# A hybrid decoder step on one core: routing on the unnormalised rows, and a different split of the last additions

## What is computed

```
xp = xp + merge_branches(...)                       # x1: residual + output projection (@ w_out)
h  = rms_norm(xp, g_ffn) = xp * rsqrt(mean(xp^2) + eps) * g_ffn
logits = h @ w_router + b_router                    # 1024 -> 32 experts
top_v, top_e = top_k(logits, 4); gates = softmax(top_v)
y = sum over the 4 chosen experts of gate * (clamped SwiGLU(h @ w_gu[e] + b_gu[e]) @ w_down[e] + b_down[e])
xp = xp + y
y_out = rms_norm(xp, g_final)
```

## Time and profile before

| | |
|---|---|
| median of 3 runs (lowest to highest) | 1586.99 us (1584.3 to 1587.69) |
| the profiled execution, its own time | 1584.94 us |
| its span, first to last instruction | 1583.1 us |
| PE busy | 1541.8 us (97%) |
| DVE busy | 790.7 us (50%) |
| ACT busy / POOL busy | 277.6 us (18%) / 186.9 us (12%) |
| DMA | 509.52 MB, mean 322 GB/s |
| mean granted TensorE clock | 0.987 |

### The profile page before, as it was taken

How to read it: one execution, slowest core, us unless ns; L and a number is a source line. 1 busy time by engine, 2 the same in 40 slices (tenths; PEclk the granted TensorE clock), 3 DMA queues, 4 the chain that set the end, 5 groups by cost and what they waited for, 6 DMA issues and landing times.

```text
span 1583.1 us, 32897 instructions
## 1 busy us (share of the span) xinstructions
PE 1541.8 (97%) x13183; PEld 713.7 (45%) x13183; DVE 790.7 (50%) x2042; ACT 277.6 (18%) x554; POOL 186.9 (12%) x269
## 2 busy tenths in 40 slices
PE   9999999999999799999999999999999999999995
PEld 8677487777755433333333333333333333333332
DVE  4349738704523645444544454445444534453448
ACT  2310020005301111111111121111111111111113
POOL 3633410014200000000000000000000000000000
PEclk9999999999999799999999999999999999999998
DMA  6555755723170599999999999999999999999995
GB/s 238 163 166 171 254 183 172 249 84 127 40 304 29 194 376 416 417 420 410 417 414 416 413 416 416 417 403 416 415 413 402 414 415 417 406 416 417 416 400 201
DMA packets 72468, 509.52 MB, mean 322 GB/s; under 512 B 13338, under 2 KB 13786, under 8 KB 47186
## 3 DMA queue, kind: packets, MB, share of 16 engines
q1 hardware_dynamic: 62154, 489.15, 77.3%
q0 software_dynamic: 10256, 19.61, 3.6%
HBM read 497.50 MB, written 19.88 MB: 327 GB/s over the span
## 4 chain that ended last, share of the span: by engine, by line
PE 77%; DMA 17%; DVE 2%; issue 1%; ACT 1%; POOL 1%; SPq 0%; DVEq 0%; POOLq 0%; ACTq 0%
PE PS L1319 36%; PE PS L935 16%; DMA weight_ring<-w_gu 16%; PE PS L1325 7%; PE PS L1243 3%; PE PS L1331 3%; PE PS L986 2%; PE PS L1051 2%; PE PS L1037 1%; PE PS L1101 1%; PE PS L1000 1%; POOL weight_ring L629 1%; DVE weight_ring L1804 1%; PE PS L1276 1%; DMA y_k<-region_x,idx_y 1%
## 5 line engine op out<-in xcount | busy, mean ns | idle before, releaser
L1319 PE MATMUL PS<-weight_ring,region_experts 128*32 128x512 f32 x5376 | 596.9, 593 | 6.7 <-DMA weight_ring<-w_gu 5.8
L1319 PEld LDWEIGHTS PS<-weight_ring,region_experts 128*32 128x32 f32 x5376 | 170.0, 110 | 400.6 <-issue 365.2
L1738 DVE TENSOR_TENSOR region_experts<-PS,region_w 128x512 f32<-128x512 f32 x96 | 66.4, 692 | 459.1 <-PE PS L1319 459.1
L1325 PE MATMUL PS<-weight_ring,act_turned 128*32 128x512 f32 x2048 | 225.6, 592 | 0.0
L935 PE MATMUL PS<-region_x,region_w 128*128 128x260 f32 (+1 forms) x928 | 209.4, 385 | 1.0 <-DVE region_x L1542 1.0
L935 PEld LDWEIGHTS PS<-region_x,region_w 128*128 128x128 f32 x928 | 175.2, 190 | 33.1 <-issue 4.6
L1729 DVE STREAM_TRANSPOSE region_experts<-region_x 32x256 f32<-32x256 f32 x372 | 161.2, 433 | 4.7
L862 ACT ACTIVATE region_experts<-region_experts 128x256 f32<-128x256 f32 x96 | 40.0, 416 | 620.8 <-DVE region_experts L1740 620.8
L1325 PEld LDWEIGHTS PS<-weight_ring,act_turned 128*32 128x32 f32 x2048 | 66.6, 110 | 153.2 <-issue 153.2
L1331 PE MATMUL PS<-weight_ring,act_turned 128*32 128x256 f32 x2048 | 118.1, 383 | 3.0 <-DVE act_turned L1750 3.0
L667 POOL DMA_INDIRECT y_k<-region_x,idx_y x32 | 30.0, 938 | 678.4 <-ACT region_x L885 602.7
(11 more groups left out here) (277 smaller groups left out, 1119.6 us busy)
## 6 DMA issues: line engine op xcount, KB each, us to landing
weight_ring<-w_gu SPq DMA_DIRECT2D x112, 2048.0 KB, 12.0
weight_ring<-w_down SPq DMA_DIRECT2D x64, 2048.0 KB, 12.3
ring_more<-w_gu SPq DMA_DIRECT2D x16, 2048.0 KB, 21.6
region_w<-w_mt SPq DMA_DIRECT2D x33, 512.0 KB, 4.2
weight_ring<-cache_kT SPq DMA_DIRECT2D x64, 256.0 KB, 4.1
weight_ring<-cache_v SPq DMA_DIRECT2D x64, 256.0 KB, 3.8
weight_ring<-w_out SPq DMA_DIRECT2D x2, 2048.0 KB, 10.8
weight_ring<-y_k SPq DMA_DIRECT2D x2, 2048.0 KB, 12.5
```

The lines of the kernel that those rows point to most:

```text
L1319: mm = pe.matmul(bank(g)[GRP * q:GRP * q + GRP], hTe[u][:, k, GRP * g:GRP * g + GRP], weights(k // 2, u)[:, k % 2, SEG * q:SEG * q + SEG], ...
L1325: mm = pe.matmul(bank(3)[GRP * j:GRP * j + GRP], actT[:, kk, GRP * g:GRP * g + GRP], w_dn[:, kk, 512 * h:512 * h + 512], start=(kk == 0), ...
L1738: dve.tensor_tensor(gu, bank(g), b_wide, ALU.add).then_inc(S["biased"], 1)
```

## The change

It has two parts.

*Routing.* The router weights are multiplied once by `g_ffn` (`wr_scaled`), TensorE turns x1 itself instead of `hf(t)`, and 1/rms is applied to the 32 logits in `find`. So the turn waits for x1 and not for the norm. For the last tile ScalarE does the copy of the turned rows before square and root, and VectorE does `find` before it writes `hf(t)`. The turn and routing of the second-last tiles move from behind the last tile's projection into it, all of the ranks but the last follow it at once, and VectorE's `find` and its share of the rank numbers (`choice_ranks`) for them come ahead of the last x1. `keep_clock` puts products of constants into TensorE's waits: 2, 4, 5, 5 and, while the first gather is under way, 12. `turn_gates` and `pick_gates_first` move from before expert 0 into its first round, after four of its eight steps, and expert 0 does not wait for `zero_late` any more.

*End.* Rank 0 is no longer added to x1 by VectorE; TensorE adds x1 to the same PSUM sums by a product with the identity (`x1_into`). The samples lie as four quadrants of 256 columns (partitions 32q to 32q + 7), so their sum of squares needs a product with `same32` across partitions, and their final norm works on 256 columns. Samples and ranks are all added after the last expert's rounds. The copy of the sample sums back (`ys_back`) goes.

```diff
@@ TensorE, routing
-                pe.wait_ge(S["hf_done"], n + 1)
+                pe.wait_ge(S["dve_taken"], KD + n + 1)
-                    ... transpose(..., hf(t)[0:r, P * k:P * k + P], ident[0:r, 0:r])
+                    ... transpose(..., xn(t)[0:r, P * k:P * k + P], ident[0:r, 0:r])
+            def keep_clock(times):
+                for _ in range(times):
+                    pe.matmul(bank(0, P), ones[:, :], ones[:, :], start=True, stop=True)
+            pe.wait_ge(S["wr_scaled"], 1)
             for n, t in enumerate(WO_ORDER):
...
+                if n == NTILE - 1:
+                    out_half(n, 0, range(4))
+                    hf_turn(n - 1)
+                    route(n - 2)
+                    out_half(n, 0, range(4, KD))
+                    route(n - 1)
+                    mm = out_half(n, 1, range(KD))
...
-            rank(0)
-            rank(1)
-            route(NTILE - 2)
+            for n in range(NTILE - 1):
+                rank(n)
+            pe.wait_ge(S["dve_taken"], KD + NTILE - 1)
+            keep_clock(2)
             hf_turn(NTILE - 1)
+            keep_clock(4)
             route(NTILE - 1)
-            rank(2)
-            rank(3)
+            keep_clock(5)
             rank(NTILE - 1).then_inc(S["rank_ready"], 1)
+            keep_clock(5)
@@ TensorE, experts
+                        if lead and u == 0 and k == 3:
+                            turn_gates()
+                            pick_gates_first()
...
+                    if lead and u == 0:
+                        pe.wait_ge(S["gT_done"], 1)
...
                     pick_rows_first()
-                    turn_gates()
+                    keep_clock(12)
...
                 turn_rows_first(b * (NE // 2 + 1) + 1)
-                    pick_gates_first()
-                    pe.wait_ge(S["zero_late"], 1)
+                    pair(b, 0, first, lead=True)
@@ TensorE, end
+            def x1_into(t, g):
+                for a in range(2):
+                    pe.matmul(GB[g][:, a, :], ident, xn(t)[:, 512 * a:512 * a + 512], start=True, stop=False)
+            def last_into(t, g):
+                for a in range(2):
+                    mm = pe.matmul(GB[g][:, a, :], back[:, t, :], y_last[:, 512 * a:512 * a + 512], start=False, stop=True)
+                mm.then_inc(S["gb_ready"], 1)
+            x1_into(2, 0)
+            x1_into(3, 3)
             pe.wait_ge(S["y_ready"], NE + 1)
+            for q in range(4):
+                if q == 2:
+                    pe.wait_ge(S["y_rest"], 1)
+                mm = pe.matmul(bank(2, 256)[32 * q:32 * q + 32], back[:, 4, 0:32], y_last[:, 256 * q:256 * q + 256], ...)
+            mm.then_inc(S["gb_ready"], 1)
+            last_into(2, 0)
+            last_into(3, 3)
+            x1_into(0, 2)
+            last_into(0, 2)
+            pe.wait_ge(S["fin_sq"], 1)
+            pe.matmul(bank(3, 1), same32, rms2[:, 4:5], start=True, stop=True).then_inc(S["fin_ss"], 1)
+            pe.wait_ge(S["fin_gb"], 2)
+            x1_into(1, 0)
+            last_into(1, 0)
@@ ScalarE
                 if n == NTILE - 1:
                     hfT_out(n - 1)
+                    hfT_out(n)
@@ VectorE, routing
-                dve.tensor_tensor(rt_log[0:r, t, :], bank(4 + n % 2, NE)[0:r], rt_br[0:r], ALU.add)
+                dve.scalar_tensor_tensor(out=rt_log[0:r, t, :], in0=bank(4 + n % 2, NE)[0:r],
+                                         scalar=rms[0:r, t:t + 1], in1=rt_br[0:r], op0=ALU.mult, op1=ALU.add)
+            dve.tensor_tensor(wr_sb[:, :, :], wr_sb[:, :, :], gffn_col..., ALU.mult).then_inc(S["wr_scaled"], 1)
+                if o == NTILE - 1:      # before the wait for the last projection
+                    for m in (2, 3):
+                        find(m)
+                        add_before(m)
+                    choice_ranks(0, 3)
+                    choice_ranks(4, 5)
...
+                norm(o)
+                if o == NTILE - 1:
+                    find(o)
                 norm_rows(o)
-                for m in ((), (), (0,), (1,), (2, 3))[o]:
+                for m in ((), (), (0,), (1,), ())[o]:
@@ VectorE, end
-                    if last and u == 1:
-                        add_samples(0)
-                        add_rank(0, 0)
+            def add_ranks(again):       # after the last pair
+                add_rank(1, again)
+                add_samples(again)
+                add_rank(2, again)
+                add_rank(3, again)
@@ SyncE, end
-                for k in range(TOPE):
-                    sp.dma_start(ys[:, k, :], ...)
-                sp.dma_start(ys[:, TOPE, :], ...)
+                for q in range(4):
+                    sp.dma_start(ys[32 * q:32 * q + NS, 0:TOPE, :], rows).then_inc(S["ys_in"], 16)
+                    sp.dma_start(ys[32 * q:32 * q + NS, TOPE, :], x1_tail[:, 256 * q:256 * q + 256]).then_inc(S["ys_in"], 16)
...
+            for q in range(4):
+                sp.dma_start(gfin4[32 * q:32 * q + 32], g_final[256 * q:256 * q + 256].partition_broadcast(32)).then_inc(S["late_in"], 16)
```

More of the change, by code:

```diff
@@ L54 @@
 PICK = 8
-SUMS = 4 * TOPE
+SUMS = 4 * (TOPE - 1)
 YROWS = NTILE * P
@@ L81, in build_step @@
 def build_step(nc, xT, xnat, consts, g_mix, w_mt, w_v, w_mix, pool_scale, w_bra, w_brp, w_out,
-               w_router, b_router, b_gu, w_gu, w_down, b_down, g_ffn, g_final, bias_strip, bias_s, bias_n,
+               w_router, b_router, b_gu, w_gu, w_down, b_down, g_ffn, g_ffnT, g_final, bias_strip, bias_s, bias_n,
                cache_kT, cache_v, cache_kiT, page_table, state, stateT,
@@ L254, in build_step @@
         yk = [part(W7, 0, 4, D) if k == 1 else part(W6, slot((2, 0, 3, 4)[k]), 4, D) for k in range(TOPE)]
-        yf = [yk[0][:, t, :] if t < 4 else part(WR, 0, D) for t in range(NTILE)]
-        ys = part(X2, 2400, TOPE + 1, 64)
+        yf = [yk[0][:, t, :] for t in range(4)]
+        ys = part(X2, 2400, TOPE + 1, 256)
+        gfin4 = part(X2, 3680, 256)
         junk = part(W6, slot(5), D)
@@ L278, in build_step @@
         unused = [small(211 + n) for n in range(2)]
+        gffn_col = small(214, KD)
         top_v = part(WR, 3936, NTILE, 8)
@@ L1333, in down_rest, with pair @@
                 return mm
-            def pair(b, i, first=False, last=False):
+            def pair(b, i, first=False, last=False, lead=False):
                 for u in range(2):
@@ L1377, in experts @@
                 if first:
-                    pick_gates_first()
-                    pe.wait_ge(S["zero_late"], 1)
-                with pe.Fori(0, NE // 2 - 1 if first else NE // 2) as i:
+                    pair(b, 0, first, lead=True)
+                with pe.Fori(1 if first else 0, NE // 2 - 1 if first else NE // 2) as i:
                     pair(b, i, first)
@@ L1581, in _, with norm @@
                 dve.tensor_tensor(sga[:, d, META:NT], sga[:, d, META:NT], sbb[:, d, META:NT], ALU.add).then_inc(S["m_done"], 1)
-            def norm_rows(n):
+            def norm(n):
                 t = WO_ORDER[n]
@@ L1587, in norm_rows @@
                 L(dve.reciprocal(rms[0:r, t:t + 1], rms[0:r, t:t + 1]))
+            def norm_rows(n):
+                t = WO_ORDER[n]
+                r = TROWS[t]
                 dve.scalar_tensor_tensor(out=hf(t)[0:r], in0=xn(t)[0:r], scalar=rms[0:r, t:t + 1], in1=gffn[0:r],
@@ L1787, in add_samples @@
             def add_samples(again):
-                dve.wait_ge(S["ys_in"], 16 * (TOPE + 1) * (again + 1))
+                dve.wait_ge(S["ys_in"], 16 * 8 * (again + 1))
                 for k in range(TOPE):
@@ L1818, in last_pair @@
                 pair(0, NE // 2 - 1, True, True)
-                for k in range(1, TOPE):
-                    add_rank(k, 0)
+                add_ranks(0)
             experts(0, True)
@@ L1926 @@
         "g_ffn": x["g_ffn"][0],
+        "g_ffnT": x["g_ffn"][0].reshape(KD, P).T,
         "g_final": x["g_final"],
```

117 lines of the change are left out of this document (56 added, 61 removed).

## The result

| | before | after |
|---|---|---|
| median (lowest to highest) | 1586.49 us (1584.3 to 1587.69), 4 runs | 1598.08 us (1596.96 to 1598.9), 4 runs |
| ratio, with its 95% interval | | 1.0078 [1.0066, 1.0091] |
| the profiled execution / its span | 1584.94 / 1583.1 us | 1598.49 / 1596.6 us |
| expert 0 starts its first round | 538.25 | 545.10 |
| expert 0 starts its second round | 545.57 | 556.85 |

The changed kernel is slower, as forecast, by 11.6 us instead of 4.4, and lies 2.1 us above the range. The last four rows split the span: start and end lost 11.3 and 2.8 us, and the stream of weights between them took the same time (997.5 and 997.0).

A forecast was written before the change was run, and what follows sets the result against it. TensorE and DMA were taken to bind the experts together, so only the weight stream's start and end could move. Start +5.9 and end -1.5 gave +4.4 us: 1591.4 on the median, range 1583.5 to 1596.

The forecast's parts named there:

- The gap before TensorE's last products: TensorE between the last `down_rest` and its last products, beyond a branch: idle 2.30 us again, as before.
- the end: From the last expert's `down_wide` on: a gain of 1.5 us, with bounds of 0 and 3.7.
- The first gather beside the queue: Issued at 528.6 amid `w_down`, it takes 10.1 us for 3.8 before (bounds 3.8 and 10.8), landing at 538.7.
- the last x1: Last projection on TensorE: starts 3.4 us later, at 516.05, by scaled router weights and work moved inside it.
- low clock of expert 0: Expert 0 starts at half clock after TensorE's silence: costs 1.3 us, bounds 0 and 3.
- The rival of the free gather: First gather not held up by `w_down`, landed at 532.8: 1583.5 us in all; chance 0.25.
- the absorbed delay: Rival: TensorE waits less for `w_gu`, so only the end's gain is left: 1585.5 us; chance 0.15.
- The three parts put inside the projection: Turn of the samples 0.6, a routing 1.8, samples' routing 0.6: they put off the last x1 by 3.0 us.
- The row numbers: Expert 0's row numbers, after the routing: out at 527.5, 1.8 us earlier than before.
- the rival of the lost clock: TensorE's clock is lost in the routing, 2.6 us later for the same rest: 1594 us; chance 0.17.
- that wait costs nothing: Wait for `h_rows` ahead of the first gather: landed 2.9 us after 525.0, so no cost before issue at 528.6.
- The gates: Turning and picking the gates now stand inside expert 0's first round: +1.7 us.

The follow-up runs named there:

- after_again: The changed kernel run again, unchanged, as a yardstick: 1597.35 us, 1.0082 of the kernel before.
- s_end: The kernel before with only the end part of the change, its routing kept: 1588.47 us, 1.0018 of the kernel before.
- b_wet: The kernel before with `w_down` issued late, some 2 us ahead of the first gather: 1592.32 us, 1.0043 of the kernel before.
- a_late: The changed kernel with turns and routings of the second-last tiles back behind the last projection: 1597.50 us, 1.0081 of the kernel before.
- s_start: The kernel before with only the routing part of the change, its end kept: 1597.14 us, 1.0079 of the kernel before.
- a_dry: The changed kernel with `w_down` issued only when the first gather has landed: 1591.53 us, 1.0035 of the kernel before.
- a_noconst: The changed kernel without any of its 28 products of constants: 1597.60 us, 1.0074 of the kernel before.
- e_nobranch: The kernel before with the end part of the change, without TensorE's branch over further passes: 1583.34 us, 0.9987 of the kernel before.
- e_ahead: The kernel before with the end part, the first two tiles' x1 products ahead of TensorE's branch: 1587.80 us, 1.0014 of the kernel before.
- b_const_dry: The kernel before with constants in TensorE's waits and `w_down` behind the first gather: 1584.94 us, 0.9988 of the kernel before.
- mix_n: The kernel before plus constants, `w_down` behind the gather, the new end with `same32` ahead of tile 0's products, no TensorE branch: 1585.65 us, 0.9997.
- b_const: The kernel before with products of constants in TensorE's waits (4, 5, 4, 5, and 16 at the gather): 1585.18 us, 0.9995.

## Why the prediction was right and wrong

**What failed.** Two terms were sized too small. The gap before TensorE's last products was put at 2.30 us and was 5.50, and with the clock that fell beside it (0.55 granted in its second half) the end went from -1.5 to +2.8. The first gather beside the queue was put at 10.1 us and was 11.6. The rest of the miss at the start, +11.3 for +5.9 in this trace and +7.3 in after_again, is the last x1 and the low clock of expert 0 (0.59 granted over its first 32 records), and it varies with the execution. That the gather would be slow beside `w_down`, and that a gap would stand before those products, was right; the sizes were not. By the medians the forecast missed by 7.2 us, and the end's terms are 4.3 of that in this trace.

**Right in kind.** `w_down` and the gather side by side, a start at low clock (6.12 us for 32 records that take 3.64 at 1.00), the stream late by as much, `down_rest` in 3.64 us with no idle time before it, and a wait of VectorE ahead of the samples' scaling are all in the trace. The rival of the free gather fell (11.6 us, and 11.2 to 12.0 in the six other runs that issue it beside `w_down`), as did that of the absorbed delay (997.0 us of weights for 997.5, and no shorter for the late starts than for the early ones). One of the rivals' sums has a slip: with the end's gain of 3.7 the free gather gives 1582.1, not 1583.2.

**The last x1: 516.05 forecast, 518.09 found.** The three parts put inside the projection cost nearly what was forecast: from its first record to x1 it took 14.1 us in s_end, b_wet and a_late and 17.4 in after_again, s_start, a_dry and a_noconst, 3.3 for 3.0. In this trace the clock comes on top, which fell inside that projection: 0.62 granted in the stretch, with TensorE busy all through, and 5.38 us for eight records that took 3.68 in after_again.

```profile
505.10:508.00 2.90, 2.90 (x6) 1.26 (x6) 1.73 (x8) 0.00 (x0) 0.00 (x0) 0.62 0.01 3
```

after_again shows 515.34, so the fallen clock was one execution's. That 515.34 lies so near the forecast says little, as x1 moves by 2 us between traces of the same code. Work in 32 columns and transposes stands just before that stretch in both, so what decides is open. That scaling the router weights costs 0.4 us held: the last projection's first record is at 498.56 before and at 498.98 here.

**The row numbers: out at 527.5 forecast, 529.40 and 526.64 found.** Behind x1 the forecast had 11.45 us; both traces have 11.3. This step held. The clock did too: turn in 1.04 and routing in 1.97, both at a granted clock of 1.00, so the rival of the lost clock fell. No run shows the 521.95 that the sums take for the end of the routing, 5.9 us behind x1; the routing ended at 523.95, also 5.9 behind an x1 that came 2.0 later. Whether a turn alone would hold the clock is not shown, as ranks or routings stand right before every turn that kept it (1.06 us in a_noconst, 1.09 in a_late).

**The first gather: landed 538.7 forecast; 542.62 and 539.8 found.** This step was sized too small. Its time beside the queue is 11.2 to 12.0 us, where I took 10.1 from the gathers of the steady state. And "that wait costs nothing" was wrong by 0.6: `h_rows` landed at 530.1, after 2.9 us as forecast, but from there to the issue GpSimd took 0.93 us as well; behind the row numbers of 529.40 the issue was due at 530.5 and came at 531.05.

**Expert 0: from its start to its second round +3.0 forecast, +4.4 and +3.3 found.** The gates cost 1.7 as forecast (551.06 to 552.79). The low clock cost 2.5 (6.12 at 0.59 granted for 3.64 at 1.00) where I had 1.3. With the parts above this makes +11.3 us at r1 in the first trace, +7.3 in the second, for +5.9. By the medians the start costs 12.0 us (s_start against the runs of before beside it) and the gather's place 5.2 to 6.6 of them (a_dry); in this trace the gather itself is 7.8 us longer (11.6 for 3.8). How the remaining microseconds divide between the other terms varies with the execution and is not settled.

**The end: -1.5 forecast, +2.8 found.** Counted from `down_wide`, `down_rest` ends after 10.5 us, forecast and found. Then the gap: 2.30 taken from the earlier trace rows, 5.50 found. This was the step of the end that failed. In the trace of before, the gap stood where the DMA had run dry (share 0.39 and 0.00 from 1557 to 1561). Now it comes with the queue full:

```profile
1565.00:1567.00 2.00, 0.00 (x0) 0.00 (x0) 1.97 (x4) 1.94 (x4) 0.00 (x0) 1.00 1.06 403
1567.00:1569.00 2.00, 0.00 (x0) 0.00 (x0) 1.93 (x4) 0.80 (x2) 0.00 (x0) 0.58 0.98 394
```

The DMA view of 1564 to 1570 has instruction packets among the data (packets, MB, share):

```profile
q8 instruction: 2, 0.03, 2.7%
```

The clock fell beside it: 1.00 granted in the first half of the gap, 0.55 in the second and 0.63 in the first eight x1 records, which took 5.83 us, for 3.70 at 1.00 in e_nobranch, which has no gap. From TensorE's start to `same32` it took 13.3 us for 12.1. So 3.2 + 1.2 = 4.4 us, against 4.3 of error. By that the root came at 1583.43, and not VectorE but TensorE's order set the end. VectorE's own chain was 1.8 us late too, as `yk[1]` needed 12.7 us for 11.0. e_nobranch measures that bound: no gap is worth 2.1 us against before in the stage (37.9 for 40.0), where I had 3.7.

**Not asked at all.** The prediction costed the delayed `w_down` as a given of the change. One moved wait on SyncE (a_dry) would have shown that the change and its largest cost are separate.

## What to carry to other kernels

When a producer is moved later, list every transfer behind it in its queue and what small transfer that a chain waits for they will now meet (3.8 us for the gather alone, 11.6 beside `w_down`); a bulk load whose data is needed late can wait for that small one. Price a stall from a row with the same DMA load, not only the same code: the gap's size came from a row with a drained queue (2.30 us at a DMA share of 0.03, for 5.50 at 1.01). Behind a branch over the code of further passes put no work on the path that ends last, if it can stand elsewhere, and don't hope that work ahead of the branch will hide the gap (e_ahead: 1.77 and 3.13 us behind it, for 4.99 in s_end); what part the amount of code plays was not tried.

## What the runs showed of the hardware

- A branch over the code of further passes left TensorE idle 4.8 to 6.1 us with the queue full or nearly so (share of 0.72 or more in either half of the gap, ten traces), 2.3 to 3.2 us when the queue had drained (before, b_wet, s_start, b_const_dry) and not at all without the branch (e_nobranch, mix_n). In b_const the gap was 5.1 us although the queue was full only as it began (share 0.77 at 1556, 0.16 at 1557, then 0.00 until 1560.79). That code is fetched there and waits behind the data is the author's reading and not shown: q8, which the profile calls instruction, moved 2 packets from 1564 to 1570 in after, and one from 1552 to 1556 in mix_n, which has no gap.
- A gather of 96 rows of 4 KB took 3.7 to 3.9 us alone and 11.2 to 12.0 beside 4 MB just issued. In the trace of after each queue moved 16 packets between 537 and 538, 0.26 MB for the loads and 0.07 for the gather, and 34 each between 538 and 540. The gather's first packet came over 4 us after its issue there, for 1.6 in a_dry; no run shows the cause.
- Products of constants in TensorE's waits changed no median measurably: 1597.60 without and 1597.35 with them in the changed kernel, where the gather ends last, and 0.9995 [0.9985, 1.0005] when added to the kernel before (b_const).
